# Preparing the first weight pair of each part on VectorE between output tiles, in a two-layer decoder step on one core

## The reference, cut to what matters

```python
def swiglu(h, w_in, w_out):
    a, b = jnp.split(h @ w_in, 2, axis=-1)
    return (jax.nn.silu(a) * b) @ w_out
...
x = x + 0.5 * swiglu(rmsnorm(x, g_ffa[i]), w_ffa_in[i], w_ffa_out[i])
h = rmsnorm(x, g_mix[i])
...
x = x + mix
x = x + 0.5 * swiglu(rmsnorm(x, g_ffb[i]), w_ffb_in[i], w_ffb_out[i])
gate = jax.nn.sigmoid(rmsnorm(x, g_ple[i]) @ w_ple_gate[i])
x = x + gate * (ps[g][i] @ w_ple_proj[i])
```

## Time and profile before

| | before |
|---|---|
| median of the runs | 2741.33 us |
| the profiled execution's own time | 2743.89 us |
| its span, first to last instruction | 2742.2 us |
| PE busy | 2528.1 us (92%) |
| DVE busy | 1713.1 us (62%) |
| ACT busy | 1023.4 us (37%) |
| POOL busy | 694.6 us (25%) |
| mean granted clock of TensorE | 0.963 |

### The profile page before, as it was taken

The page is one execution under the profiler, slowest core; times in us unless marked ns, Lnnn a source line. Parts: engine busy times, 40 slices in busy tenths (PEclk is TensorE's granted clock), DMA queues, the critical chain, the costliest instruction groups (busy, mean ns, idle before and its releaser), DMA issues.

```text
span 2742.2 us, 45352 instructions
## 1 busy us (share of the span) xinstructions
PE 2528.1 (92%) x17541; PEld 2395.5 (87%) x17541; DVE 1713.1 (62%) x2326; ACT 1023.4 (37%) x1707; POOL 694.6 (25%) x416
## 2 busy tenths in 40 slices
PE   4999998999899899999997999998999989999988
PEld 4999988876688899898986989898987889898978
DVE  6827367788554883645778637278334696372786
ACT  4525242344233352433234425252134244252422
POOL 2040322212330503223232140503322321405032
PEclk9999999999899999999998999999999999999998
DMA  3323223122232133222222323233323223232322
GB/s 98 92 77 92 83 83 81 41 50 78 67 111 60 54 93 90 79 82 79 80 66 72 92 72 97 62 91 79 93 54 97 81 77 93 76 92 62 91 72 65
DMA packets 410793, 216.25 MB, mean 79 GB/s; under 512 B 40085, under 2 KB 407834, under 8 KB 410650
## 3 DMA queue, kind: packets, MB, share of 16 engines
q1 hardware_dynamic: 404646, 209.17, 27.4%
q0 software_dynamic: 3584, 1.84, 0.4%
q10 hardware_dynamic: 2420, 3.37, 0.4%
HBM read 206.57 MB, written 7.76 MB: 78 GB/s over the span
## 4 chain that ended last, share of the span: by engine, by line
PE 71%; DVE 14%; issue 5%; POOL 5%; ACT 4%; DMA 1%; DVEq 0%; SPq 0%; ACTq 0%; POOLq 0%
PE ps L2431 11%; PE ps L2433 11%; PE ps L2432 11%; PE ps L2374 9%; PE ps L2379 9%; PE ps L2376 9%; PE ps L995 2%; DVE x L2193 1%; DVE st L613 1%; DVE xh L2080 1%; PE ps L909 1%; POOL g2f L1753 1%; POOL wlo L1740 1%; DVE ub L2191 1%; DVE r L2059 1%
## 5 line engine op out<-in xcount | busy, mean ns | idle before, releaser
L1729 POOL TENSOR_TENSOR wlo<-raw,whi 128x1024 fp32r<-128x1024 f32 (+2 forms) x175 | 404.4, 2311 | 1648.8 <-ACT whi L1804 1648.8
L1804 ACT ACTIVATE whi<-raw 128x1024 fp32r<-128x1024 f32 (+2 forms) x175 | 169.5, 968 | 534.6 <-PE ps L2379 509.9
L2374 PE MATMUL ps<-uh,whi 128*128 128x320 f32 (+1 forms) x1408 | 304.5, 298 | 17.8 <-DVE x L2193 10.9
L2376 PE MATMUL ps<-ul,whi 128*128 128x320 f32 (+1 forms) x1408 | 302.8, 296 | 0.0
L2379 PE MATMUL ps<-uh,wlo 128*128 128x320 f32 (+1 forms) x1408 | 302.7, 296 | 0.0
L2191 DVE TENSOR_TENSOR ub<-ps,r 128x576 f32<-128x576 f32 x96 | 72.5, 755 | 298.1 <-PE ps L2379 298.1
L2374 PEld LDWEIGHTS ps<-uh,whi 128*128 128x128 f32 x1408 | 217.3, 190 | 21.9 <-ACT whi L1804 15.7
L2116 DVE TENSOR_TENSOR wlo<-raw,whi 128x1024 fp32r<-128x1024 f32 x76 | 101.0, 1329 | 191.9 <-ACT whi L1820 191.9
L2376 PEld LDWEIGHTS ps<-ul,whi 128*128 128x128 f32 x1408 | 217.3, 190 | 0.0
L2379 PEld LDWEIGHTS ps<-uh,wlo 128*128 128x128 f32 x1408 | 217.2, 190 | 0.0
L2374 PE MATMUL ps<-xh,whi 128*128 128x320 f32 x752 | 167.0, 304 | 16.2 <-DVE xl L2073 8.4
(11 more groups left out here) (430 smaller groups left out, 7394.4 us busy)
## 6 DMA issues: line engine op xcount, KB each, us to landing
raw<-in_w_ffa_in SPq DMA_DIRECT2D x88, 512.0 KB
raw<-in_w_ffb_in SPq DMA_DIRECT2D x88, 512.0 KB
raw<-in_w_ffa_out SPq DMA_DIRECT2D x32, 512.0 KB
pages<-in_cache_ckv SPq DMA_DIRECT2D x128, 128.0 KB, 2.0
raw<-in_w_ffb_out SPq DMA_DIRECT2D x32, 512.0 KB
raw<-in_w_mlstm_in SPq DMA_DIRECT2D x24, 512.0 KB
raw<-in_w_ple_gate SPq DMA_DIRECT2D x16, 512.0 KB
raw<-in_w_ffa_out SPq DMA_DIRECT2D x16, 384.0 KB
```

The costliest lines, as they stand in the source:

```text
L1729: pool.tensor_tensor(lo[:, 0:n, :], raw[:, p % RAW, 0:n, :], hi[:, 0:n, :].bitcast(F32), ALU.subtract).then_inc(wlo_ready, 1)
L1804: act.activation(hi[:, 0:n, :], raw[:, p % RAW, 0:n, :], ACT.Copy).then_inc(whi_ready, 1)
L2374: mm(out[:, t], hi[:, n, :], xh_n[:, t], start=first and n == 0, stop=False)
L2376: mm(out[:, t], hi[:, n, :], xl_n[:, t], start=False, stop=False)
```

## The change

It has five parts.

1. `PARTS` becomes `[(0, 6), (6, 14), (14, 22)]`: the first part has six pairs and six-chunk output tiles, the last has eight.
2. POOL's `first_pair` goes. DVE prepares pair 0 of a later part between output tiles: the sums after tile 4, the lowers 2 and 3 after tile 5, the lowers 4 and 1 after tile 6. For the first part of an FFN the same steps stand between the chunks in `added`, `ple` and the start. ACT makes the uppers of pair 0 at the matching places: the second and third ahead of the upper of output panel 7, the fourth and first behind it. SP loads the two panels of pair 0 each as its own slot is free, not both when both are.
3. In the last part's `ffn_out`, ACT writes x times the gain (`x_scaled_upper`) and the squares (`x_squares`); DVE keeps the lower and the sum. ACT does both for every tile, after the tile is in x. The preparations of FFN inputs likewise take the scaled chunk from ACT (`x_scaled`, `x_upper_b`), and DVE forms its sums with scalar_tensor_tensor straight from x.
4. The output tiles wait for `out_read` (DVE has read tile k-2 out of PSUM) in place of `tile_taken` (x is updated).
5. The silu of pair 0 of an FFN's first part (`gate`) moves behind the first copy of pair 1. At the start, the squares of the input move from ahead of pair 0 to between its copies.

```diff
-PARTS = [(0, 8), (8, 16), (16, 22)]
+PARTS = [(0, 6), (6, 14), (14, 22)]
...
+        order = (1, 2, 3, 4) if i else (2, 3, 4, 1) if self.q else (2, 1, 3, 4) if self.f % 2 else (1, 2, 3, 4)
+        return 4 * (self.g0 + i) + order.index(n) + 1
...   # SP, ffn
+                        for s in (0, 1):
+                            last = max([p for p in range(8, part.p) if p % RAW == h + s], default=0)
+                            if i < 2 and last:
+                                sp.wait_ge(wlo_ready, last - 7)
...   # POOL, ffn
                 for part in PART[f]:
-                    first_pair(part)
                     for k in range(8):
                         lower(part.p + k, 0, part.n)
...   # ACT, ffn
                         copied(part, i, 1, 1, B, A)
+                        if i == 1 and part.q == 0:
+                            gate(part, 0)
...
+                        if i or part.q:
+                            gate(part, i)
                     u_upper(part, part.n - 1)
                     upper(part.p + 1, 0, part.n)
...
+                        for k in range(2, 8):
+                            if k == 7:
+                                second_upper(after, 0)
+                                third_upper(after, 0)
+                            upper(part.p + k, 0, part.n)
+                        fourth_upper(after, 0)
+                        first_upper(after, 0)
                     else:
-                        upper(part.p + 8, 0, last_upper)
+                        for k in range(8):
+                            if k < 6:
+                                upper(part.p + 2 + k, 0, part.n)
+                            elif k == 6:
+                                upper(part.p + 8, 0, last_upper)
+                            act.wait_ge(tile_taken, part.t + k + 1)
+                            x_scaled_upper(nxt, k)
+                            x_squares(nxt, k)
...   # DVE, ffn_out
+                for c in range(NC_D):
+                    dve.wait_ge(panel_used, part.p + c + 1)
+                    dve.wait_ge(tile_taken, part.t + c)
+                    dve.tensor_tensor(ub[:, :], slot(part.t + c, bank), r[:, :], ALU.mult).then_inc(out_read, 1)
+                    dve.wait_ge(out_read, NC_D * part.k + c + 1)
+                    dve.scalar_tensor_tensor(out=x[:, c, :], in0=ub[:, :], scalar=-0.5, in1=x[:, c, :], op0=ALU.mult,
+                                             op1=ALU.add).then_inc(tile_taken, 1)
+                    if name:
+                        if c:
+                            x_sum(name, c - 1)
+                        dve.wait_ge(tile_taken, part.t + c + 1)
+                        x_scaled_lower(name, c)
+                    elif c == 4:
+                        second_sums(after, 0)
+                        third_sums(after, 0)
+                    elif c == 5:
+                        second_lower(after, 0)
+                        third_lower(after, 0)
+                    elif c == 6:
+                        fourth_lower(after, 0)
+                        first_lower(after, 0)
...   # DVE, added
                     x_blocks(f, c)
+                    if c == 5:
+                        second_sums(part, 0)
+                        third_sums(part, 0)
+                    if c == 6:
+                        second_lower(part, 0)
+                        first_lower(part, 0)
+                third_lower(part, 0)
                 for k in range(4):
                     x_third_lower(f, k)
+                fourth_lower(part, 0)
...   # PE, ffn
+                    with pe.Fori(1, NC_D // 2) as i:
                         for k in (0, 1):
-                            pe.wait_ge(tile_taken, part.t + k - 1 + i * 2)
+                            pe.wait_ge(out_read, NC_D * part.k + k - 1 + i * 2)
```

More of the change, by code:

```diff
@@ L148, in hybrid_step @@
         gn = whole.put("gn", [P, NG])
+        gneg = whole.put("gneg", [P, 4, 4])
         cf = whole.put("cf", [P, NCF])
@@ L1855, in u_upper, with gate, ffn @@
                 act.activation(uh[:, i, :], ub[:, :], ACT.Copy).then_inc(uh_done, 1)
-            def ffn(f, norm, last_upper):
+            def gate(part, i):
+                g = part.g0 + i
+                act.wait_ge(w_act, 2 * g + 2)
+                if g:
+                    act.wait_ge(w_ub, g)
+                act.activation(sA[:, :], tA[:, :], ACT.Silu).then_inc(silu_done, 1)
+            def ffn(f, norm, last_upper, nxt):
                 for part in PART[f]:
@@ L1861, in ffn @@
                         A, C, B, D_ = [ps[:, part.bank(i) + k, 0:HT] for k in range(4)]
+                        embed = not part.k and not i
                         if i:
@@ L1882, in ffn, with x_scaled_upper @@
                         copied(part, i, 4, 5, D_, B)
[L1883 removed]
+                        if embed:
+                            embed_square(4)
                             root(norm, D, bank=1)
[L1885 to L1888 removed]
+                        if i or part.q:
+                            gate(part, i)
                     u_upper(part, part.n - 1)
                     upper(part.p + 1, 0, part.n)
[L1891 to L1892 removed]
                     if part.q < 2:
[L1894 to L1896 removed]
+                        after = PART[f][part.q + 1]
+                        for k in range(2, 8):
[5 more added lines that the diff above has]
+                        first_upper(after, 0)
+                    else:
+                        for k in range(8):
[6 more added lines that the diff above has]
+                            x_squares(nxt, k)
+            def x_scaled_upper(name, c):
+                g = gn[:, GCOL[name] + c:GCOL[name] + c + 1]
+                dst = xh2 if name[0:3] == "ple" else xh
+                act.activation(dst[:, c, :], x[:, c, :], ACT.Copy, scale=g).then_inc(xh_act, 1)
             def x_squares(name, c):
@@ L2114, in first_lower @@
                 s = part.slot(i)
-                dve.wait_ge(g_hi, 4 * (part.g0 + i) + 1)
+                dve.wait_ge(g_hi, part.uppers(i, 1))
                 dve.tensor_tensor(wlo[:, s, :, :], raw[:, 2 * part.half(i), :, :], whi[:, s, :, :].bitcast(F32),
@@ L2128, in fourth_lower @@
             def fourth_lower(part, i):
-                dve.wait_ge(g_hi, 4 * (part.g0 + i) + 4)
+                dve.wait_ge(g_hi, part.uppers(i, 4))
                 dve.tensor_tensor(blocks(g4l), raw_pair(part, i)[:, 3, :], blocks(g4h).bitcast(F32),
@@ L2492, in pair @@
                               False, True)
-                pe.wait_ge(g_hi, 4 * g + 4 + dyn * 4)
-                if first and not e:
-                    pe.wait_ge(first_lo, part.lowered(0, 4))
-                else:
-                    pe.wait_ge(g_lo, part.remainders(e, 4) + dyn * 4)
+                pe.wait_ge(g_hi, part.uppers(i, 4) + add)
+                pe.wait_ge(g_lo, part.remainders(i, 4) + add)
                 pe.wait_ge(w_copied, 4 * g + 4 + dyn * 4)
```

338 lines of the change are left out of this document (145 added, 193 removed).

## The result

The changed kernel takes 2581.61 us (median of four runs, 2580.45 to 2582.94) against 2741.33: a ratio of 0.9418, with a 95% interval of 0.9402 to 0.9435. That is 160 us less. 2600 was forecast, with a range of 2575 to 2640: the sign and the size are right, and the forecast was 18 us too high.

What follows compares the result with a forecast made beforehand. PE, busy 92% of the span, was taken as the bound, so only closing its gaps or restoring its clock pays. Gains of 71.8 + 43.7 + 27 = 142.5 us off 2743.89 gave 2601.4, stated as 2600, range 2575 to 2640.

Steps and rivals of the forecast that it cites:

- Part A: Later parts' pair 0: preparation fits between output tiles, so the eight gain 80.0 us, 71.8 after delays at output panel 7.
- Panel 7: Output panel 7's upper queues behind pair 0's: 0.4 us late in three aligned FFNs (1.2), 7 us in the fourth.
- a wait of 2 to 4 us at tile 7: Sign expected in the trace: PE waits on the lower at output tile 7, in the fourth FFN alone.
- DVE and POOL in each other's way: A DVE instruction begun during one of POOL loses up to 2 us, once; POOL loses less than 0.5 us.
- Part B: Last parts' tiles run without gaps (29.3 us) and the following stages start sooner (14.4): 43.7 us in all.
- the embedding stages' panel 1 late: After the second and fourth FFN, ACT issues five loads before panel 1's upper, so the panel comes 1.7 us late.
- Part C: The FFNs' own starts: DVE takes over POOL's work; 5.5, 5.5, 6 and 10 us, 27 in all.
- only moves the stall two products on: FFN starts, pair 1: moving gate frees one copy but the third still waits, so the 2.0 us stall only shifts.
- The squares at the start: First FFN's start: input squares no longer hold pair 0's copies in one piece; this start's gain 10 us, least certain.
- the band of 2585 to 2620: The forecast's narrower range for the whole kernel's time in us, given a chance of 0.65.
- everything hidden: Rival for the whole kernel: all three gains at full size, 80 + 46 + 40, giving 2575 us; chance 0.12.
- The slower rival: Pair 0's load delays output panel 7 at eight seams; a loss from 17.8 us later on; chance 0.03, slower or same.

Runs made afterwards that it cites:

- prep_late: The changed kernel, but DVE prepares the later parts' pair 0 only after output tile 7, ACT's uppers behind all panels'; 2652.85 us, ratio 0.9689.
- pad64: The kernel before the change with only an unused 64-byte buffer added behind the gains, shifting all buffers behind it; 2723.53 us, ratio 0.9949.
- pad128: The kernel before the change with an unused 128-byte buffer in the same place behind the gains; 2723.29 us, ratio 0.9946.
- pad_uh: The kernel before the change with 64 unused bytes ahead of uh, moving only uh, ul and what lies behind; 2728.70 us, ratio 0.9971.
- cut_back: The changed kernel with the parts cut as before, eight, eight, six; ACT keeps the scaled uppers and squares; 2576.50 us, ratio 0.9399.

## Why the prediction was right, and what it missed

**Part A, the later pair 0s** (80.0 said, 80.0 measured, before what panel 7 takes back). Right, and prep_late shows the cause: the place under the tiles.

**Panel 7** (1.2 + 7 us said, 13.3 measured). The mechanism and its places are right, in both kinds of FFN, and the chain's times nearly so, with one link exchanged for another in the aligned ones (above). The term was mis-sized. In the aligned FFNs PE wants the panel at 9.5, not 9.6, and its gap of 0.85 where 0.4 was taken comes with other small losses to 1.1 us a part. In the fourth FFN's first part the load came at 7.0 (6.9 said) but POOL ended 0.8 us later than said (14.0 against 13.2); in the second the load came at 8.0, where 8.1 was said (the 4.2 and 4.1 us given for it add up to 8.3); and the clock after the gap of 4.64 was priced at about 1 us in all where the first part alone lost 7.0 - 4.6 = 2.4. As a sign, a wait of 2 to 4 us at tile 7 was named, in the fourth FFN alone; it was 4.6 and 2.9 there, and 0.85 in the other three.

**DVE and POOL in each other's way.** `g3l` began 0.61 us after POOL's lower at 145.10 and took 2.86 us where 1.23 is its length; it ended 1.1 us after POOL did. `g4l`, the next lower, took its own 0.69. That is the charge that the prediction made, once per instruction of POOL; it fell a second time in this part, on the first sum at 139.75 (0.7 us), and not on the update of x. POOL's lower of 768 columns took 2.38, where the first of the same part (at 116.11) took 1.84: 0.5 us lost, not 1.3. It began at 145.10 while DVE's `g2l` (144.57 to 145.79) still ran, so it lost about what was left of that one, 0.69, and not a whole lower. By the rule of the Trainium skill ("SBUF — State Buffer", "Who interferes with whom") DVE is held to the end of POOL's instruction, 147.48, and then needs 1.23, which gives 148.71 as an estimate; the trace has 148.57 and agrees.

**Part B** (43.7 said). The last parts' tiles run without a gap, as said (29.3), and the stages behind them gave 15.8 (14.4 said), with the embedding stages' panel 1 late by 1.0 and 1.3 us where 1.7 was counted. The reason given was the DVE's count, six instructions to four, "5.1 of 6.40 us": true as a sum, but it read two edits as one. The experiments show that either the new cut or ACT's share is enough, so each is worth nothing once the other is there, and that a third of what the six-chunk tiles lost (2.3 of 6.7 us) goes neither with the one nor the other.

**Part C, the FFN starts** (27 said, 36.4 measured). Mis-sized in each: 32.75 where 35.5 was said, 39.38 where 42 was, 60.19 where about 61 was (69 less the window's start at 8.27), 32.60 where 35.5 was. In the second FFN PE stood for 3.15 us for the first lower (4.2 said) and had no wait at the third lower (2.4 said): DVE's queue was read as too long. That the moved `gate` "only moves the stall two products on" is nearly so: 0.2 to 0.7 us an FFN at a like clock. But the changed kernel's profiled execution had the clock at 1.00 in all three such pair 1s, where other traces of the same order have 0.89 and 1.0 us more in some; up to 3 us of the 36.4 are of this kind. The squares at the start, the least certain term, are worth some 5 by the windows.

**Not in the prediction at all: the placement of the buffers.** The faster 320-column matmuls gave 8 x 0.64 = 5.1 us in the eight-chunk tiles, and the 8 us that lie elsewhere agree with the 9 that the same stretches lose in pad64. Alone, in the kernel before, they are worth 14 us (pad64 by its ratio: 0.51% of 2741). So some 13 of the 18 us come from a term that the prediction didn't have. Without it the result would have fallen near 2595 by this estimate (2581.6 + 13), 5 us below the forecast and in the band of 2585 to 2620.

**The balance of the 18.4 us** (160.9 against 142.5): panel 7 -5.1; tiles +4.9 over what was said; stages behind them +1.4; starts +9.4; elsewhere +7.8; sum 18.4. That the range held owes something to luck: the result came within 7 us of its low end, which stood for everything hidden (80 + 46 + 40), though panel 7 was not hidden but cost more than said; the placement, which no part of the count had, made up for it. The slower rival never came near: it needs loads 17.8 us later than counted, and in the fourth FFN they were within 0.1 us of it.

## What to carry to other kernels

Work that an engine does in a seam between two stages belongs under the stage before it: here the same work on DVE was worth 71 us under the tiles, and behind them it took as long as POOL's. When such work is put into a queue, put it behind the operand that the running stage still needs, not ahead: panel 7's upper first was worth 9 to 11 us for a swap of three lines. And when a change also allots a buffer, time the old kernel with that buffer alone before explaining a gain. A difference that shows in PE's clock in one profiled execution should be looked for in other traces of the same order before it is put down to the edit.

## What the runs showed of the hardware

- The same matmuls on the same data take another time by where their moving operand lies in SBUF (pad64, pad128, pad_uh). Moved by 64 bytes, 320 columns go from 149 to 145.5 ns and 256 stay at 117.5; by 128 bytes, 140 and 120. An eight-chunk part takes 51.20, 50.56 and 49.94 us, and the whole kernel 0.5% less in either case.
- A stall of PE can cost more than its length, where the clock falls behind it: in the fourth FFN's first part 4.64 us of gap at tile 7 went with 7.0 us of loss and a granted clock of 0.92; in prep_late pair 0 took 13.16 in place of 11.14 behind a wait of 8.5.
- The same stall doesn't always cost the same. In eight-chunk tiles of the fourth FFN a wait of 2.9 us cost 3.1 at a clock of 1.00 (the changed kernel), and one of 2.8 cost 4.6 at 0.97 (cut_back). The same pair 1 with small gaps takes 13.95 us at 1.00 or 14.92 at 0.89, in one order of the code, from FFN to FFN and trace to trace.
- DVE's and POOL's instructions on SBUF hold each other up: DVE's `g3l` took 2.86 us for 1.23 when begun 0.61 us after POOL's lower, and POOL's lower 2.38 for 1.84 when begun during DVE's `g2l`.
